# One channel tile of all 2048 columns as the unit of W1, in the experts of a hybrid layer

## What is computed

```
h = x @ w1[e] + b1[e]              # (block, 1024) @ (1024, 2048)
glu, lin = h[..., ::2], h[..., 1::2]
glu = min(glu, 7); lin = clip(lin, -7, 7)
a = glu * sigmoid(1.702 * glu) * (lin + 1)
y = a @ w2[e] + b2[e]              # (block, 1024) @ (1024, 1024)
out[token] += gate * y
```

## Time and profile before

| | |
|---|---|
| median of 3 runs | 1616.1 us (1615.35 to 1617.4) |
| the profiled execution, its own time | 1607.52 us |
| its span, on which all rows stand | 1605.7 us |
| first part, until the experts start | some 447 us |
| the 32 experts, 447 to 1585 us | some 1138 us |
| TensorE busy, of the span | 1555.1 us (97%) |
| VectorE, ScalarE, GpSimd busy | 1330.1, 1010.7, 606.1 us |
| weights and all else moved | 466.69 MB |

### The profile page before, as it was taken

The page is one execution under the profiler, slowest core; times in us unless marked ns, Lnnn a source line. Parts: engine busy times, 40 slices in busy tenths (PEclk is TensorE's granted clock), DMA queues, the critical chain, the costliest instruction groups (busy, mean ns, idle before and its releaser), DMA issues.

```text
span 1605.7 us, 24420 instructions
## 1 busy us (share of the span) xinstructions
PE 1555.1 (97%) x8474; PEld 1266.0 (79%) x8474; DVE 1330.1 (83%) x1161; ACT 1010.7 (63%) x881; POOL 606.1 (38%) x429
## 2 busy tenths in 40 slices
PE   9999999989989999999999999999999999999994
PEld 7777788775668788888888888888888888888873
DVE  5599755552689899999999999999999999999895
ACT  5434343211457777777777777777777777777774
POOL 5643641422331223443344343333334333433331
PEclk9999999999999999999999999999999999999997
DMA  6322101111589999999999999999999999999995
GB/s 189 110 79 80 15 14 54 54 54 37 210 318 338 392 372 377 386 385 377 388 380 382 371 386 384 379 384 378 377 383 387 385 369 381 382 376 387 386 378 166
DMA packets 146633, 466.69 MB, mean 291 GB/s; under 512 B 21031, under 2 KB 35021, under 8 KB 146574
## 3 DMA queue, kind: packets, MB, share of 16 engines
q1 hardware_dynamic: 136766, 436.84, 71.6%
q0 software_dynamic: 9664, 28.53, 7.6%
q10 hardware_dynamic: 144, 0.52, 0.1%
HBM read 443.15 MB, written 22.71 MB: 290 GB/s over the span
## 4 chain that ended last, share of the span: by engine, by line
PE 77%; DVE 12%; DMA 7%; ACT 2%; issue 2%; SPq 0%; DVEq 0%; POOLq 0%; ACTq 0%; POOL 0%
PE banks L1763 19%; PE banks L1765 19%; PE banks L1764 19%; DMA slots<-in_expert_w_dram 5%; PE banks L1708 2%; DVE lo L2121 2%; PE banks L1772 2%; PE banks L1792 1%; PE banks L1758 1%; PE banks L1498 1%; PE banks L1383 1%; DMA x_sum<-xs 1%; PE banks L1384 1%; PE banks L1385 1%; PE banks L1561 1%
## 5 line engine op out<-in xcount | busy, mean ns | idle before, releaser
L2121 DVE TENSOR_TENSOR lo<-slots,hi 128x2048 fp32r<-128x2048 f32 x384 | 862.5, 2284 | 45.2 <-PE banks L1765 27.3
L1151 ACT CAST hi<-slots 128x2048 fp32r<-128x2048 f32 x384 | 734.5, 1913 | 249.2 <-DMA slots<-in_expert_w_dram 159.5
L1763 PE MATMUL banks<-lo,x_hi 128*128 128x512 f32 x1040 | 411.9, 396 | 0.1
L1765 PE MATMUL banks<-hi,x_lo 128*128 128x512 f32 x1040 | 406.8, 391 | 0.0
L1764 PE MATMUL banks<-hi,x_hi 128*128 128x512 f32 x1040 | 406.4, 391 | 0.0
L937 POOL DMA_INDIRECT x_sum<-hT,idy x32 | 112.3, 3508 | 476.5 <-ACT hT L1247 460.8
L1765 PEld LDWEIGHTS banks<-hi,x_lo 128*128 128x128 f32 x1040 | 195.9, 188 | 41.7
L1763 PEld LDWEIGHTS banks<-lo,x_hi 128*128 128x128 f32 x1040 | 196.0, 188 | 39.7 <-DVE lo L2121 0.3
L1764 PEld LDWEIGHTS banks<-hi,x_hi 128*128 128x128 f32 x1040 | 196.2, 189 | 39.5
L1763 PE MATMUL banks<-lo,a_hi 128*128 128x512 f32 x496 | 194.4, 392 | 3.0 <-DVE lo L2121 3.0
L1764 PE MATMUL banks<-hi,a_hi 128*128 128x512 f32 x496 | 193.7, 391 | 0.0
(11 more groups left out here) (383 smaller groups left out, 1932.3 us busy)
## 6 DMA issues: line engine op xcount, KB each, us to landing
slots<-in_expert_w_dram SPq DMA_DIRECT2D x384, 1024.0 KB, 11.1
slots<-in_w_in_dram SPq DMA_DIRECT2D x13, 1024.0 KB, 5.1
xs<-in_x_dram SPq DMA_DIRECT2D x8, 512.0 KB, 5.6
slots<-in_w_out_dram SPq DMA_DIRECT2D x2, 2048.0 KB, 9.1
x_sum<-xs SPq DMA_DIRECT2D x4, 512.0 KB, 9.4
h_rows<-slots SPq DMA_DIRECT2D x4, 512.0 KB, 3.4
xs<-x_sum SPq DMA_DIRECT2D x4, 512.0 KB, 4.8
x_sum<-xs POOLq DMA_DIRECT2D x3, 512.0 KB, 10.2
```

The costliest lines, as they stand in the source:

```text
L1151: nc.scalar.copy(w_hi[n % HI][:, :, :], raw[r]).then_inc(hi_ready, 1)
L1763: nc.tensor.matmul(out, x_h, w_l, start=first, stop=False)
L1765: return nc.tensor.matmul(out, x_l, w_h, start=False, stop=last)
L2121: tensor_tensor(w_lo[n % LO][:, :, :], raw[n % RAW], w_hi[n % HI][:, :, :], ALU.subtract).then_inc(lo_ready, 1)
```

## The change

The unit of W1 becomes one channel tile of all 2048 columns, so unit k of W1 holds rows k·128 to k·128+127 in full, with one run of 8192 bytes per row in place of two of 4096. Each unit writes all four banks 2 to 5. None of them is complete before u = 7. So the four bias products stand ahead of unit 0, both sigmoids and both halves of `swiglu` wait for unit 7 (ScalarE: after u = 10; VectorE: after u = 10 and after u = 11), and TensorE waits at unit 0 until both halves of the hidden row of the block before were read. The product of the overflow counts moves from bank 4 to bank 0.

```
 def load_w1(eng, e, k, n):
-    o, k = k // 4 * 2 * CW, k % 4 * 2
-    eng.dma_start(raw[n % RAW].rearrange("p (k c) f -> p k (c f)", k=2),
-                  W1_T[:, bass.ds(e, 1), k:k + 2, o:o + 2 * CW].rearrange("p a k f -> p (a k) f"))\
+    eng.dma_start(raw[n % RAW].rearrange("p c f -> p (c f)"),
+                  W1_T[:, bass.ds(e, 1), k:k + 1, :].rearrange("p a k f -> p (a k f)"))\
...
 def sigmoid(i, n, b, p):
-    wait_used(act, i, n + 4 * p + 3)
+    wait_used(act, i, n + W1U - 1)
...
 # ScalarE, block_work
-    if u == 6:
-        sigmoid(i, q * UNITS, b, 0)
     if u == 10:
-        sigmoid(i, q * UNITS, b, 1)
+        for p in range(2):
+            sigmoid(i, q * UNITS, b, p)
...
 # TensorE, w1_unit
-    half = u // 4
-    if u % 4 == 0:
-        for c in range(2):
-            nc.tensor.matmul(bank[2 + 2 * half + c], sel[:, q, c, :], b1r[:, half, :], start=True, stop=False)
-    for k2 in range(2):
-        k = u % 4 * 2 + k2
-        for c in range(2):
-            ins = three_products(bank[2 + 2 * half + c], x_hi[:, k, :], x_lo[:, k, :],
-                                 w_hi[n % HI][:, 2 * k2 + c, :], w_lo[n % LO][:, 2 * k2 + c, :], k == KT - 1)
+    if u == 0:
+        for b in range(4):
+            nc.tensor.matmul(bank[2 + b], sel[:, q, b % 2, :], b1r[:, b // 2, :], start=True, stop=False)
+    for b in range(4):
+        ins = three_products(bank[2 + b], x_hi[:, u, :], x_lo[:, u, :],
+                             w_hi[n % HI][:, b, :], w_lo[n % LO][:, b, :], u == KT - 1)
...
 # TensorE, block_work
-    pe.wait_ge(hid_free, b * 2 - 1)
+    pe.wait_ge(hid_free, b * 2)
     for k in range(W1U):
-        if k == 4:
-            pe.wait_ge(hid_free, b * 2)
...
 # VectorE, block_work
-    if u == 2 and overflow:
+    if u == 0 and overflow:
         overflow_tables()
     if u == 5:
         act_low(b - 1)
-        wait_used(dve, i, q * UNITS + 3)
-        swiglu(b, 0)
-    if u == 9:
+    if u >= 10:
         wait_used(dve, i, q * UNITS + W1U - 1)
-        swiglu(b, 1)
+        swiglu(b, u - 10)
...
 # VectorE, first block
-wait_used(dve, 0, FIRST + 3)
+wait_used(dve, 0, FIRST + W1U - 1)
 swiglu(0, 0, True)
```

More of the change, by code:

```diff
@@ L1298, in _ @@
                     act_high(0)
-                if u == 6:
-                    sigmoid(0, UNITS, 1, 0)
                 if u == 10:
-                    sigmoid(0, UNITS, 1, 1)
+                    for p in range(2):
+                        sigmoid(0, UNITS, 1, p)
             x_high(2)
@@ L1325, in _ @@
                             high_part(i, n + u)
-                            if u == 6:
-                                sigmoid(i, n, b, 0)
                             if u == 10:
-                                sigmoid(i, n, b, 1)
+                                for p in range(2):
+                                    sigmoid(i, n, b, p)
                                 x_high(b + 1)
@@ L1799, in block_work @@
                 pe.wait_ge(sel_set, b + 1)
-                pe.wait_ge(hid_free, b * 2 - 1)
+                pe.wait_ge(hid_free, b * 2)
                 for k in range(W1U):
-                    if k == 4:
-                        pe.wait_ge(hid_free, b * 2)
+                    if k == 0 and overflow:
+                        overflow_rows()
+                    w1_unit(i, q * UNITS + k, k, q)
+                    if k == 1:
                         if overflow:
                             pe.wait_ge(tables_ready, 1)
[L1806 to L1810, removed]
                         act_transposes(b - 1)
@@ L1830, in first_block @@
                 pe.wait_ge(sel_set, 2)
-                pe.wait_ge(hid_free, 1)
+                pe.wait_ge(hid_free, 2)
                 for k in range(W1U):
-                    if k == 4:
-                        pe.wait_ge(hid_free, 2)
                     w1_unit(0, UNITS + k, k, 1)
@@ L1850, in overflow_rows @@
                 pe.wait_ge(ovf_diag_ready, 1)
-                nc.tensor.matmul(bank[4][:, 0:2 * E], ones_b[0:E, :], ovf_diag[:, :, :].rearrange("p n e -> p (n e)"),
+                nc.tensor.matmul(bank[0][:, 0:2 * E], ones_b[0:E, :], ovf_diag[:, :, :].rearrange("p n e -> p (n e)"),
                                  start=True, stop=True).then_inc(ovf_full, 1)
@@ L2357, in overflow_tables @@
                 dve.wait_ge(ovf_full, 1)
-                ps = bank[4]
+                ps = bank[0]
                 step(nc.vector.tensor_copy(blkexp[:, :], ps[:, E:2 * E]))
@@ L2392, in _ @@
                     act_low(0)
-                    wait_used(dve, 0, UNITS + 3)
-                    swiglu(1, 0)
                 if u == 8:
                     overflow_blocks()
-                if u == 9:
+                if u >= 10:
                     wait_used(dve, 0, UNITS + W1U - 1)
-                    swiglu(1, 1)
+                    swiglu(1, u - 10)
             x_low(2)
@@ L2421, in _ @@
                             low_part_of(i, n + u)
-                            if u == 5:
-                                wait_used(dve, i, n + 3)
-                                swiglu(b, 0)
                             if u == 9:
                                 wait_used(dve, i, n + W1U - 1)
-                                swiglu(b, 1)
+                                for p in range(2):
+                                    swiglu(b, p)
                                 x_low(b + 1)
```

## The result

| | before | changed |
|---|---|---|
| median of 4 runs | 1615.7 us (1615.0 to 1617.4) | 1661.6 us (1658.6 to 1666.8) |
| ratio, 95% interval | | 1.0291 [1.0274, 1.0308] |
| profiled execution, own time | 1607.5 us | 1666.8 us |
| its span | 1605.7 us | 1665.0 us |

The profiled execution of the changed kernel is the longest of its four; that of the kernel before is none of its four and shorter than each. The change costs 45.9 us between the medians. The prediction said 1657 us, within 1638 to 1680.

What follows compares the result with a forecast made beforehand. TensorE sets the pace, VectorE and DMA close behind, VectorE with 0.07 us margin at block starts. Terms sum to +45.2 us on the profiled 1607.5, 1652.7; the middle of 1653 and 1661 gives 1657 us, range 1638 to 1680.

Steps and rivals of the forecast that it cites:

- The steady blocks: Starts of blocks 4 to 31: TensorE waits 1.30 us for VectorE's low part at each of 28, +36.4 us.
- The back payment: Blocks 3 to 31: time now lost to late loads is given back, since the loader gets 1.3 us more per block, -2.6 us.
- Longer rows do not free VectorE: Rival, chain from u = 8 to next u = 0: longer rows ease SBUF, no stall, 1615 us or less; chance 5%.
- Half a stall: Rival, steady block starts: the loader slows VectorE less, stall 0.7 us, 17 us less, 1640 us; chance 8%.
- The clock stays at 1.00: Judges a rival: TensorE's clock falls at each block-start stall, 48 us more, 1705 us; chance 7%.
- Longer rows are not slower: Judges a rival on W1's loads: longer rows slower by over 3%; at 6%, 25 us more, 1682 us; chance 4%.
- Block 0 to 1: VectorE's first swiglu half waits for the eighth unit, table load and sigmoid, starting 7.1 us later: +7.1 us.
- block 1: Block 1 to block 2: a 2.0 us half moves into VectorE's gapless stretch, u = 8 starts 0.3 us earlier: +1.7 us.
- Block 2 and 3: Block 2 to 3 gets the 1.3 us stall but loses a 2.08 us late-load wait and 1.7 us slow clock: +1.3 - 3.8 us.
- so both go: Block 2 to 3: loads have up to 7 us more, so the late-load wait and slow clock vanish, -3.8 us.
- The end: Block 31: transposes wait for the second swiglu half, +3.4 us, and TensorE runs at half clock after idling, +1.7 us.
- the second reading: Whole run: the 8.6 us of median above profile are not late loads that VectorE's stalls cover, giving 1661 us.

Runs made afterwards that it cites:

- the second experiment: The kernel before with only W1's loads changed to rows of 8192 bytes, output not the layer's: 1609.62 us, ratio 0.9969.
- the second pair: Both kernels unchanged, profiled once more side by side: 1609.24 us before, 1656.57 us changed.
- the first: The original profiled executions of both kernels: 1607.5 us before, 1666.8 us changed.
- The sixth experiment: The changed kernel with block 31 alone rewritten, both sigmoids behind u = 9 and both swiglu halves ahead of u = 10's low part: 1656.41 us, ratio 1.0251.
- the second comparison: Both kernels unchanged, run again as single executions on a third chip: changed 1656.57 us, before 1609.24 us (profiled) and 1608.66 us.

## Why the prediction was right, step by step

**The steady blocks.** Predicted 1.30 us at each of 28 starts, measured 36.28 - 35.02 = 1.26. The cause was shown from three sides: the order alone makes the same loss, taking 0.8 us out of the chain leaves 0.46 us, taking out more leaves nothing. The back payment was right as well: blocks 4 to 30 took 948.14 us before, which is 2.6 us more than 27 periods of 35.02, and between 600 and 1500 us no load is late any more.

**The rivals.** Longer rows do not free VectorE: its low part takes 2.29 us as before. Half a stall did not happen either, at 368 GB/s it is the same 2.29. The clock stays at 1.00 through stalls of 0.96 us. The Trainium skill's warning of an unsteady clock when PSUM banks are cycled through ("TensorE: Matmul & The Clock Gate", "A second HAM failure mode: psum-queue depth-cycling") does not appear with four banks in turn. Longer rows are not slower but a little faster: the Trainium skill's fixed overhead per packet ("DMA: Bandwidth & Descriptors", "Why small descriptors are slow") has the sign that the second experiment shows, 0.3% less time; how much of it comes from there, no run tells.

**Block 0 to 1 and block 1.** Predicted 7.1 and 1.7 us, measured 7.3 to 8.2 and 3.0. The place where it went too low is "0 to 1.7 us; I take 0" for the slow clock after the longer wait: the windows give 1.4 us, nearly the upper end. The 1.7 us of the moved half fit what is left. VectorE's way from the overflow counts of block 1 to the low part of block 2 is 14.8 us, 12.9 before (1.8 more), and ahead of the counts it gains almost nothing: ScalarE's copies of rows stand between its high parts there, and VectorE waits for those.

**Block 2 and 3.** Predicted -2.5 and +1.3, measured -2.2 and +1.1 in the second pair. In the first it was -1.5 and +2.8, by one stall of 2.03 us and the slow stretch after it. The step "so both go" was too good: TensorE's stall of 2.08 us and its slow stretch in block 2 are gone, but late loads still lengthen the stall at the start of block 3, to 1.60 or 2.03 us.

**The end.** Predicted 3.4 + 1.7, measured 5.2 in the second pair and 7.2 in the first. The wait was 3.13 us in both, and the slow clock cost 1.8 and 3.0 us. The sixth experiment takes away the wait at the transposes and the slow clock, and with them 3.8 to 5.0 us.

**The sum** of 45.2 us stands beside 45.9 between the medians (44.3 to 49.8 by the interval) and 47.3 to 47.9 in the second comparison, one execution each. In the second pair the two largest misses of a term, 1.3 us too much in the steady blocks and 1.2 too little in block 1, have opposite signs; that they cancel is luck, but the sum would hold without it. That it meets the difference of the medians within 1 us is closer than these runs can tell.

**The base.** Here the prediction was off. It took the middle of two readings of the 8.6 us by which the median lies above the first profiled execution. If they were late loads that the stalls cover, the change would have to cost some 37 us against the median. It costs 45.9, with 44.3 the lower end of the interval, and beside a kernel before of 1609 us it costs 47 to 48, from single executions. So nothing shows these microseconds coming back, and the time is that of the second reading, 1661. Where they are spent stays open: both profiles of the kernel before caught short executions, and a long one was not profiled. The long rows alone save 5.7 us in the comparison where before takes 1615 us, against 4.0 us that the blocks of the profiles account for (140.87 for 142.45 in blocks 0 to 3, 945.70 for 948.14 in blocks 4 to 30), which hints that loads have a part in it and shows no more.

## What to carry to other kernels

When a unit is cut so that all its results are complete at one time, the work that used to be spread over the block comes in one piece; add up the in-order chain from the last buffer release to the work that the next block needs, and compare it with the time until that is needed. If the margin is 0.07 us, as here, each operation placed in the chain costs nearly its whole length in every block, and each that can go behind the needed work costs nothing. A larger unit and its order are two changes: with the third operations behind the low part and the two ends rewritten, the kernel with long rows is 0.27% faster than the one before.

## What was not expected of the hardware

- Loads of 1 MB in rows of 8192 bytes land 7.1 us after their issue, those in rows of 4096 bytes 10.6 to 11.1 us, at the same 381 to 382 GB/s; ScalarE's waits for them, 129.6 us, are gone.
- A VectorE operation on 96 x 512 is followed by the next one after 0.60 us when that is independent, and after 0.78 us when it reads the result, for which it waits by a semaphore.
- An idle time of TensorE of 2.03 us was followed by a slow stretch, mean clock 0.83 over 10 us; 1.60 us at the same place in another run was not. Behind 3.13 us it fell to the lower level at once in one run and some 1.5 us later in another.
- The same code of the first part ended between 447.2 and 455.3 us in twelve profiles, 8 us, as much as single edits moved here; a stretch is better compared by its own length than by where it ends.
